# Gate table of a PEER layer: one-hot products in the split format, both gate parts in one 256-column product

## The reference

```python
    s = jnp.einsum('thpd,hpnd->thpn', q, subkeys)        # 8 heads, two halves, 128 keys each
    sv, si = lax.top_k(s, K)                             # K = 16
    ...
    best, pos = lax.top_k(cand, K)
    eidx = jnp.take_along_axis(cidx, pos, axis=-1)       # expert = i * 128 + j
    gates = jax.nn.softmax(best, axis=-1)
    act = jax.nn.gelu(jnp.einsum('td,thkd->thk', xc, u_tab[eidx]))
    w = (gates * act)
    return jnp.einsum('thk,thkd->td', w, v_tab[eidx])
```

## Time and profile before

| what | value |
|---|---|
| median of 3 runs | 989.25 us (989.06 to 989.52) |
| the profiled execution | 989.43 us |
| its span, first to last instruction | 987.7 us |
| granted TensorE clock, mean | 0.997 |
| TensorE busy | 970.7 us, 98% |
| VectorE busy | 788.9 us, 80% |
| ScalarE busy | 508.7 us, 52% |
| GpSimd busy | 372.2 us, 38% |

### The profile page before, as it was taken

How to read it: one execution, slowest core, us unless ns; L and a number is a source line. 1 busy time by engine, 2 the same in 40 slices (tenths; PEclk the granted TensorE clock), 3 DMA queues, 4 the chain that set the end, 5 groups by cost and what they waited for, 6 DMA issues and landing times.

```text
span 987.7 us, 17700 instructions
## 1 busy us (share of the span) xinstructions
PE 970.7 (98%) x6791; PEld 894.5 (91%) x6791; DVE 788.9 (80%) x1535; ACT 508.7 (52%) x731; POOL 372.2 (38%) x234
## 2 busy tenths in 40 slices
PE   8999999999999999999999999999999999999996
PEld 7999889999999999999999999888888888888884
DVE  6989888894876989987688888787876878987765
ACT  5477656555445454646444444544555555444452
POOL 1010100102888787786887756122230222200002
PEclk9999999999999999999999999999999999999998
DMA  9998958986666887886776667788889998987751
GB/s 356 413 296 282 326 168 310 331 237 214 189 184 179 194 209 179 213 196 183 180 163 159 151 172 187 269 300 291 294 278 379 302 325 326 332 277 218 219 177 42
DMA packets 87572, 239.57 MB, mean 243 GB/s; under 512 B 26945, under 2 KB 28993, under 8 KB 85825
## 3 DMA queue, kind: packets, MB, share of 16 engines
q1 hardware_dynamic: 60448, 207.94, 63.5%
q0 software_dynamic: 26752, 30.49, 13.6%
q10 hardware_dynamic: 288, 0.01, 0.0%
HBM read 227.84 MB, written 10.55 MB: 241 GB/s over the span
## 4 chain that ended last, share of the span: by engine, by line
PE 93%; DVE 3%; DMA 2%; ACT 1%; SPq 1%; POOL 1%; issue 0%; POOLq 0%; ACTq 0%; DVEq 0%
PE px L1230 35%; PE pw L907 16%; PE pw L908 16%; PE pw L909 16%; PE px L1204 3%; DMA raw<-in_w 2%; PE px L1161 1%; PE pv L907 1%; PE pv L909 1%; PE pv L908 1%; PE px L908 1%; PE px L907 1%; PE px L909 1%; DVE w_lo L1291 0%; PE px L1095 0%
## 5 line engine op out<-in xcount | busy, mean ns | idle before, releaser
L618 ACT ACTIVATE w_hi<-raw 128x1024 fp32r<-128x1024 f32 x308 | 324.7, 1057 | 301.3 <-PE px L1230 159.6
L1291 DVE TENSOR_TENSOR w_lo<-raw,w_hi 128x1024 fp32r<-128x1024 f32 x285 | 346.0, 1222 | 99.2 <-ACT w_hi L618 97.7
L907 PE MATMUL pw<-a_hi,w_hi 128*128 128x240 f32 (+1 forms) x1248 | 349.0, 280 | 0.3 <-DVE a_lo L1541 0.3
L908 PE MATMUL pw<-a_lo,w_hi 128*128 128x240 f32 (+1 forms) x1248 | 344.6, 276 | 0.0
L909 PE MATMUL pw<-a_hi,w_lo 128*128 128x240 f32 (+1 forms) x1248 | 344.6, 276 | 0.0
L571 POOL DMA_INDIRECT gates_spill<-gate,place x128 | 229.5, 1793 | 73.9 <-issue 49.3
L907 PEld LDWEIGHTS pw<-a_hi,w_hi 128*128 128x128 f32 x1248 | 236.8, 190 | 1.9 <-issue 1.2
L908 PEld LDWEIGHTS pw<-a_lo,w_hi 128*128 128x128 f32 x1248 | 236.8, 190 | 0.1
L909 PEld LDWEIGHTS pw<-a_hi,w_lo 128*128 128x128 f32 x1248 | 236.8, 190 | 0.0
L1230 PE MATMUL px<-w_hi,ws_hi 128*128 128x512 f32 x512 | 159.5, 390 | 0.0
L1230 PE MATMUL px<-w_hi,ws_lo 128*128 128x512 f32 x512 | 159.1, 389 | 0.0
(11 more groups left out here) (368 smaller groups left out, 1233.5 us busy)
## 6 DMA issues: line engine op xcount, KB each, us to landing
raw<-in_u SPq DMA_DIRECT2D x128, 512.0 KB, 4.5
raw<-in_v SPq DMA_DIRECT2D x128, 512.0 KB, 4.4
raw<-in_ws SPq DMA_DIRECT2D x52, 512.0 KB, 6.0
ada<-in_ada SPq DMA_DIRECT2D x20, 512.0 KB, 6.8
ada<-in_w_ada SPq DMA_DIRECT2D x16, 512.0 KB, 6.9
gates_spill<-zero POOLq DMA_DIRECT2D x16, 512.0 KB, 7.3
g_row<-gates_spill SPq DMA_DIRECT2D x32, 256.0 KB, 5.2
raw<-in_w SPq DMA_DIRECT2D x7, 1024.0 KB, 11.8
```

Of the source, the lines that this page charges most:

```text
L618: return nc.scalar.activation(out, in_, ACT.Copy, **kw)
L907: nc.tensor.matmul(out, lh, rh, start=start and x == 0, stop=False)
L908: nc.tensor.matmul(out, lh, rl, start=False, stop=False)
L1291: v.tensor_tensor(w_lo[:, m % RING], raw[:, m % RING], w_hi[:, m % RING].bitcast(F32), ALU.subtract).then_inc(lo_ready, 1)
```

## The change

The one-hots and the high part of the gate are exact in the split format fp32r. The change builds both one-hots of four tokens with one comparison of 1024 columns (`oh`, fp32r). ScalarE scales the one-hot of j with the high and with the low part of the gate (`g_hi`, `g_lo`), eight copies of 128 columns into every second column of `oh_g`, in a new step `gated(n)` that comes one piece after the take of group n-2. TensorE multiplies the one-hot of i with the 256 columns of `oh_g`, four products per group, into a pair of banks (`px_two[n % 2]`, so two groups in flight instead of four). VectorE adds the two parts with a reduction over pairs, in place, then copies the upper rows and multiplies the lower ones. The build of group n+2 now stands ahead of the take of group n; the build of group 1 comes two places later; POOL fetches its first row only after the last product.

```diff
@@ -52,6 +52,7 @@
 INDEX_AFTER = 39
 OH = T1 // 4
 OH_AT = [85 + 10 * n // 7 for n in range(OH)]
+GATED_AT = [OH_AT[0] - 2, OH_AT[0]] + [p + 1 for p in OH_AT[:-2]]
 GA_U = OH_AT[0] // 2
 DOT_AT = [4 + 5 * c // 2 for c in range(NS)]
 GELU_AT = DOT_AT[-1] + 1
@@ -245,8 +246,10 @@
         W = sb("W", AR, [NK, TD])
 
 
-        oh_i = [sb(f"oh_i{k}", AR + 32768 + 1024 * k, [4, P]) for k in range(2)]
-        oh_j = [sb(f"oh_j{k}", AR + 32768 + 1024 * k + 512, [4, P]) for k in range(2)]
+        oh = [sb(f"oh{k}", at, [2, 4, P], F32R) for k, at in enumerate((R0, X0))]
+        oh_g = [sb(f"oh_g{k}", at + 1024, [4, P, 2], F32R) for k, at in enumerate((R0, X0))]
+        g_hi = sb("g_hi", R0 + 2560, [P], F32R)
+        g_lo = sb("g_lo", R0 + 2688, [P])
         ws_hi = sb("ws_hi", AR + 32768, [RING, T], F32R)
         ws_lo = sb("ws_lo", AR + 33792, [RING, T], F32R)
         idx = sb("idx", AR + 34816, [3, P])
@@ -272,7 +275,8 @@
         pw = [bank("pw0"), bank("pw1")]
         pv_two = ctx.enter_context(nc.psum_tensor("pv", [P, 1024], F32))
         pv = [pv_two[:, 0:512], pv_two[:, 512:1024]]
-        px = [bank("px0"), bank("px1"), bank("px2"), bank("px3")]
+        px_two = [ctx.enter_context(nc.psum_tensor(name, [P, 1024], F32)) for name in ("px01", "px23")]
+        px = [px_two[x // 2][:, x % 2 * 512:(x % 2 + 1) * 512] for x in range(4)]
         p1 = [pw[0], pw[1], pv[0], pv[1], px[1], px[2], px[0], px[3]]
 
         def x1_columns(t, k):
@@ -579,6 +583,7 @@
             pool.wait_ge(scattered, 16 * TOPK * PH)
             pool.wait_ge(sp_landed, 32 * QUADS)
             pool.wait_ge(idxT_done, 2)
+            pool.wait_ge(oh_used, OH)
             for c in range(NS):
                 if c >= 2:
                     pool.wait_ge(sp_summed, c - 1)
@@ -837,12 +842,14 @@
                     act.wait_ge(piece_used, VP + v - RING + 1)
                 copy(ws_hi[:, v % RING, 0:TD], W[:, v]).then_inc(wsplit_hi, 1)
 
-            def take_upper(n):
-
-                act.wait_ge(oh_used, n + 1)
-                row, t = OH_AT[n] // 2 * 2, TD - 4 * n - 4
-                copy(W[:, row:NK, t:t + 4], px[n % 4][:, :].rearrange("p (t j) -> p j t", t=4)[:, row:NK]) \
-                    .then_inc(g_upper_taken, 1)
+            def gated(n):
+
+                k, t = n % 2, T1 - 4 * n - 4
+                act.wait_ge(oh_ready, n + 1)
+                for y in range(4):
+                    for x, part in enumerate((g_hi[:, :].bitcast(F32), g_lo)):
+                        last = copy(oh_g[k][:, y, :, x], oh[k][:, 1, y].bitcast(F32), scale=part[:, t + y:t + y + 1])
+                last.then_inc(oh_gated, 1)
 
             for g in range(NG):
                 if g == 8:
@@ -857,8 +864,9 @@
                 if g == INDEX_AFTER + 1:
                     act.wait_ge(idxT_done, 1)
                     copy(idx[:, :, :], pv[1][:, 0:3 * P].rearrange("p (a t) -> p a t", a=3)).then_inc(idx_ready, 1)
-                if 2 * g in OH_AT:
-                    take_upper(OH_AT.index(2 * g))
+                    copy(g_hi[:, :], pv[1][:, 2 * P:3 * P]).then_inc(idx_ready, 1)
+                if 2 * g in GATED_AT:
+                    gated(GATED_AT.index(2 * g))
                 act.wait_ge(piece_used, UP + 2 * g + 2)
                 src = pw[g % 2][:, 0:2 * TD].rearrange("p (j t) -> p j t", j=2)
                 left = TD - 4 * taken(g)
@@ -1196,13 +1204,12 @@
 
             def one_hots(n):
 
-                pe.wait_ge(oh_ready, n + 1)
-                if n >= 4:
-                    pe.wait_ge(g_lower_taken, n - 3)
-                    pe.wait_ge(g_upper_taken, n - 3)
+                pe.wait_ge(oh_gated, n + 1)
+                if n >= 2:
+                    pe.wait_ge(g_taken, n - 1)
                 for y in range(4):
-                    last = nc.tensor.matmul(px[n % 4][:, y * P:(y + 1) * P], oh_i[n % 2][:, y], oh_j[n % 2][:, y],
-                                            start=True, stop=True)
+                    last = nc.tensor.matmul(px[n % 2 * 2 + y // 2][:, y % 2 * T:(y % 2 + 1) * T], oh[n % 2][:, 0, y],
+                                            oh_g[n % 2][:, y].rearrange("p j a -> p (j a)"), start=True, stop=True)
                 last.then_inc(oh_used, 1)
 
             pe.wait_ge(keys_landed, 32)
@@ -1696,29 +1702,32 @@
 
                 k, t = n % 2, T1 - 4 * n - 4
                 if n == 0:
-                    dve.wait_ge(idx_ready, 1)
+                    dve.wait_ge(idx_ready, 2)
+                    v.tensor_tensor(g_lo[:, :], idx[:, 2], g_hi[:, :].bitcast(F32), ALU.subtract)
+                if n == 1:
+                    dve.wait_ge(idxT_done, 2)
                 if n >= 2:
                     dve.wait_ge(oh_used, n - 1)
-                v.tensor_tensor(oh_j[k][:, :, :], iota[:, :].unsqueeze(1).broadcast_to([P, 4, P]),
-                                idx[:, 1, t:t + 4].unsqueeze(2).broadcast_to([P, 4, P]), ALU.is_equal)
-                for y in range(4):
-                    last = v.tensor_scalar(oh_i[k][:, y], iota[:, :], idx[:, 0, t + y:t + y + 1], idx[:, 2, t + y:t + y + 1],
-                                           ALU.is_equal, ALU.mult)
-                last.then_inc(oh_ready, 1)
-
-            def take_lower(n):
+                full = [P, 2, 4, P]
+                v.tensor_tensor(oh[k][:, :, :, :], iota[:, :].unsqueeze(1).unsqueeze(1).broadcast_to(full),
+                                idx[:, 0:2, t:t + 4].unsqueeze(3).broadcast_to(full), ALU.is_equal).then_inc(oh_ready, 1)
+
+            def take(n):
 
                 rows, t = OH_AT[n] // 2 * 2, TD - 4 * n - 4
-                dve.wait_ge(g_upper_taken, n + 1)
+                full = px_two[n % 2]
+                g = full[:, 0:4 * P].rearrange("p (t j) -> p j t", t=4)
+                dve.wait_ge(oh_used, n + 1)
+                need(go(v.tensor_reduce(full[:, 0:4 * P], full[:, :].rearrange("p (x a) -> p x a", a=2), AX, ALU.add)))
+                v.tensor_copy(W[:, rows:NK, t:t + 4], g[:, rows:NK])
                 dve.wait_ge(u_out, OH_AT[n] // 2)
                 w = W[:, 0:rows, t:t + 4]
-                v.tensor_tensor(w, px[n % 4][:, :].rearrange("p (t j) -> p j t", t=4)[:, 0:rows], w, ALU.mult) \
-                    .then_inc(g_lower_taken, 1)
+                v.tensor_tensor(w, g[:, 0:rows], w, ALU.mult).then_inc(g_taken, 1)
 
             def gate_u(g):
 
                 dve.wait_ge(u_out, g + 1)
-                dve.wait_ge(g_upper_taken, taken(g))
+                dve.wait_ge(g_taken, taken(g))
                 w = W[:, 2 * g:2 * g + 2, TD - 4 * taken(g):TD]
                 v.tensor_tensor(w, pw[g % 2][:, 0:2 * TD].rearrange("p (j t) -> p j t", j=2)[:, :, TD - 4 * taken(g):TD], w, ALU.mult) \
                     .then_inc(u_gated, 1)
@@ -1781,12 +1790,13 @@
                     normal(1, 1)
                 if p == OH_AT[0] - 3:
                     one_hots(0)
+                if p == OH_AT[0] - 1:
                     one_hots(1)
                 if p in OH_AT:
                     n = OH_AT.index(p)
-                    take_lower(n)
                     if n + 2 < OH:
                         one_hots(n + 2)
+                    take(n)
                 if p == 2 * NG - 3:
                     dve.wait_ge(oh_used, OH)
                     v.memset(ws_hi[:, :, TD:T].bitcast(F32), 0.0)
```

More of the change, by code:

```diff
@@ L352, in layer @@
         u_out, u_gated, w_gated = sem("u_out"), sem("u_gated"), sem("w_gated")
-        oh_ready, oh_used, g_lower_taken, g_upper_taken = (sem(s) for s in (
-            "oh_ready", "oh_used", "g_lower_taken", "g_upper_taken"))
+        oh_ready, oh_gated, oh_used, g_taken = (sem(s) for s in (
+            "oh_ready", "oh_gated", "oh_used", "g_taken"))
         wsplit_hi, wsplit_lo = sem("wsplit_hi"), sem("wsplit_lo")
@@ L869, in _ @@
                 split_hi(UP + 2 * g + 5)
-                if 2 * g + 1 in OH_AT:
-                    take_upper(OH_AT.index(2 * g + 1))
+                if 2 * g + 1 in GATED_AT:
+                    gated(GATED_AT.index(2 * g + 1))
                 for n in range(2 * TT):
@@ L1189, in repeated @@
                 pe.wait_ge(gate_exp, 2 * TT)
-                pe.wait_ge(idx_ready, 1)
+                pe.wait_ge(idx_ready, 2)
                 for k in range(KC):
@@ L1237, in v_ready @@
                 pe.wait_ge(wsplit_lo, v + 1)
-            pe.wait_ge(g_lower_taken, OH)
-            pe.wait_ge(g_upper_taken, OH)
+            pe.wait_ge(g_taken, OH)
             for v in range(NK - RING):
```

## The result

The changed kernel takes **991.85 us** (median of 12 runs, 991.37 to 992.17); the kernel before took 989.41 us (12 runs, 989.02 to 989.98) in the same comparison. The ratio is 1.0024, with an interval of 1.0015 to 1.0033. So the change costs 2.4 us, 0.24%, where 1.05 us less were forecast. The profiled execution has a span of 990.2 us, against 987.7 before, at a granted clock of 0.995: the same 2.5 us are in the trace.

A forecast was written before the change was run, and what follows sets the result against it. VectorE was to become the bound: 24 groups (73.7), 32 splits (36.5) and 17 gatings (2.7), 112.9 us to 601.75, then 12.2 us of TensorE. Piece 124 starts 1.1 us earlier, forecasting 988.2 us against 989.25; range 981 to 1003.

The forecast's parts named there:

- 24 x 3.07: VectorE's 24 groups up to place 117: build 1.14, reduction 1.25, copy 0.19, multiplication 0.49 us each, together 73.7 us.
- the multiplication at 0.49: VectorE's multiplication of the lower rows in each take: 0.49 us on the mean of the first 24, as before.
- the copy behind the reduction: In VectorE's take: the copy waits for the reduction's end and starts 0.03 us after it, so the reduction occupies 1.25.
- TensorE is the bound again from piece 120 on: End of the stage: after place 117 TensorE has pieces 120 to 123 and three groups, 12.2 us, starting piece 124 at 614.05.
- piece 122 against place 119: Check near the stage's end: piece 122 needs place 119, which VectorE has at 607.3; TensorE arrives at 607.7.
- The waits for scalings: TensorE at each pair of groups one piece apart: idles 0.7 us for ScalarE's scalings, which VectorE's pace covers.
- Short inner rows: Rival, the reduction in each take: pairs cost additional cycles, giving 1001 us, or 1014 at the scan's rate; chance 0.15.
- ScalarE does not bound the stage: Denies a rival in ScalarE's queue: scalings without overlap, 0.45 us each or 3.6 per group, giving 1003 us; chance 0.1.
- VectorE did not keep up: Denies a rival: a VectorE group takes 2.6 us or less, TensorE's saving arrives, less waits for scalings: 981.4 us; chance 0.12.
- The products run as one pass: Denies a rival on TensorE: 256-column products at the old type's rate, four taking 1.8 us, giving 1014 us; chance 0.02.
- PSUM as a source: Rival: VectorE's reduction and copy pay 0.107 us more each from PSUM, 5.1 us over 24 groups, 993.3 us; chance 0.03.
- A granted clock under 1.00: TensorE after its waits for the gating: a lower clock would be a cost not in the sum; no size given.

The follow-up runs named there:

- the kernel with four scalings: Against the changed kernel, ScalarE scales with the high part of the gate alone, the low part's columns staying zero: 992.37 us, ratio 1.0029 to the kernel before.

## Why the prediction was off

**The bound.** That VectorE takes over from TensorE, with a group at 3.07 us against the old 2.14, held: TensorE waits in front of even pieces for the gating, VectorE is busy 123.66 of 126.90 us, and 13.4 us of work added to TensorE cost 1.3.

**The step that failed** is the term 24 x 3.07 (73.7 us), and in it the multiplication at 0.49. That value comes from the earlier trace rows, where what follows the multiplication does not wait for it. In the change the gating does, in 14 of 24 groups, and the multiplication is 0.67 there: +2.6 us on a chain of 112.9. So a wait that the change brought in stood in the sum at nothing, and a loss came where a gain was forecast. The prediction had priced exactly this effect for the copy behind the reduction, from the earlier trace rows, and then missed the second edit of the same kind, the changed `wait_ge` in `gate_u`. It stood in the diff. Had the prediction noticed it, the 0.03 us of the earlier trace rows between the end of one operation and the start of the next would have made the multiplication 0.60 and the chain 1.5 us longer, and the forecast +0.4 instead of -1.1. Even that is short of the 2.6, since the start comes 0.10 after the end here. Taking the wait away brought the time to 988.4, and the forecast had been 988.2.

**The assumption that failed with it** is that TensorE is the bound again from piece 120 on. The prediction checked piece 122 against place 119, a margin of 0.4 us, but not piece 126 against place 123. By its own prices that place ends at 619.1 and TensorE arrives at 619.4, so the margin is 0.2 us there once VectorE's word has travelled for 0.1. The last places have two more gatings that wait for a multiplication (119 and 123, 0.18 each) and the longest gatings and multiplications. Place 123 ended 18.06 us after place 117 instead of 17.4, and TensorE stood waiting for 0.25 us. That is 0.5 us. With the 2.8 us by which place 117 is late, piece 126 starts 3.4 us later than forecast (622.79 against 614.05 + 2 x 2.68 = 619.41), and that is the distance between -1.1 and +2.4. The 2.8 us came through whole because TensorE's own way also starts from the end of place 117; no slack lies behind it.

**The other terms** were right. The products: four in 0.49 us (0.48). The reduction 1.26 (1.25), the build 1.14 (1.14), the copy 0.19 (0.19). The scalings start 0.29 us apart (0.3), as two rows of ScalarE's timeline in the changed kernel show:

```profile
490.00 0.40 ACT L623 ACTIVATE oh_g<-oh,g_hi 128x128 fp32r<-128x128 f32 x1
490.29 0.41 ACT L623 ACTIVATE oh_g<-oh,g_lo 128x128 fp32r<-128x128 f32 x1
```

The waits for scalings were to be 0.7 at pairs of groups; the longest is 0.8, 2.0 in all.

**The rivals.** Short inner rows cost nothing. ScalarE does not bound the stage: halving the scalings gains nothing, and VectorE's chain is as long without them. VectorE did not keep up, and where it was made to, the price of 981.4 was met. The products run as one pass. PSUM as a source costs no more: the reduction's 1225 ns stand beside 1220 from SBUF. The Trainium skill (VectorE: DVE Perf Modes, "The TRN2 errata") has PSUM at 120 fixed cycles against 58, an estimate of 65 ns more per operation; the reduction is 5 ns longer, so the measurement decides against it here. The slower side did come, with a chance of 0.34, but by a mechanism that no rival named. A granted clock under 1.00, which the prediction named as a cost outside its sum, came over some 3 us of the stage and lay off the chain. The rival that was missing is a wait for the operation right ahead, at 0.1 to 0.2 us for each gating.

**What stays open.** Why the wait costs 0.18 us behind a multiplication and 0.13 behind the reduction; why TensorE reaches the first group up to 0.6 us earlier in some profiles than in that of the change (487.86 to 488.49), before any of the changed products; and why the clock fell after one wait of 2 us and not after others as long (the kernel with four scalings has another of 2.1 us without a drop).

## What to carry to other kernels

Go through a diff's waits as carefully as through its operations: on a busy engine, a wait for the instruction right ahead has a price of its own, here 0.18 us each, and either waiting for an earlier producer or putting an independent instruction between the two takes it away. When a change shortens work on the engine that is the bound and adds more to the next one, add up both per period first: what counts is the second engine's order and waits from then on, and the shorter product alone was worth 1.3 of its 11.6 us. And when a forecast has the bound return to another engine, check every later place at which it could go back, and not only the first: piece 122 passed, and piece 126 cost 0.5 us.

## What the runs showed of the hardware

- A VectorE operation that waits for nothing on the one ahead starts 0.08 us before that one's end (the gating behind the multiplication of 416 elements, 558.01 + 0.58 to 558.51). One that waits for its semaphore starts 0.10 after it (560.04 + 0.58 to 560.72); the copy behind the reduction starts 0.03 after (558.60 + 1.23 to 559.86). The multiplication's occupation went from 0.485 to 0.669 us, the reduction's from 1.133 to 1.259. The first of these has an additional wait between the two instructions, for ScalarE's count, which may be where the other 0.07 us come from; that was not tried apart. The Trainium skill (VectorE: DVE Perf Modes, "The DRAIN you can't avoid") tells of copies that took the same time with a semaphore after each as with one after the last. Setting a semaphore indeed cost nothing in these runs (the copy of the upper rows occupies 0.188 us with it and 0.189 without); waiting for one did. The Trainium skill (the same page, "Rules for kernel authors") advises fewer operations rather than fewer semaphores; here the same operations with one wait moved were 3.4 us faster, and the measurement decides.
- A comparison of bf16 operands, of which one repeats in its outer dimension and runs by one inside, takes 440 ns for 512 elements, and 710 in the 32-bit form. The difference of 0.27 us is half of what 512 more elements cost in the 32-bit form (the split of 1024 takes 1240 ns in the same trace, 0.53 more than the 710), so the bf16 elements pass at twice the rate. The Trainium skill (VectorE: DVE Perf Modes, "Mode 2×_1P — pack two bf16 into one 32-bit read") asks for 16-bit types and a step of one, and the run agrees, with an inner run of only four elements.
- ScalarE writes 128 results into every second 32-bit element at no price that shows: 0.40 us long, as an activation of 128 elements that writes them side by side and has one pointer for its bias (402 ns, L748 of the changed kernel; it also adds them up).
- Two waits of TensorE of about 2 us were followed by a stretch at the lower clock level (granted clock 0.55 over 592 to 594 us in the changed kernel, 0.50 over 606 to 608 in that with four scalings); others as long were not. Products that were 0.11 us apart were 0.21 apart then.
